# Order of the first panel's products, and late mixes by GpSimd, at both feed-forward starts

## What is computed

```python
def _swiglu(h, w_gate, w_up, w_down):
    return (jax.nn.silu(h @ w_gate) * (h @ w_up)) @ w_down
...
    f = rmsnorm(h, pre_ff_g[l]) @ w_ff1[l]
    f = jnp.square(jax.nn.relu(f)) @ w_ff2[l]
    h = h + rmsnorm(f, post_ff_g[l])
```

## Time and profile before

| what | value |
|---|---|
| median of three runs | 2500.53 us (2500.17 to 2503.38) |
| the profiled execution | 2507.9 us, its span 2505.7 us |
| PE busy | 2392.7 us, 95% of the span |
| DVE busy | 1567.3 us, 63% |
| ACT busy | 1036.3 us, 41% |
| POOL busy | 258.0 us, 10% |
| chain of work that ended last | PE 66%, DVE 3%, DMA 2% |

### The profile page before, as it was taken

How to read it: one execution, slowest core, us unless ns; L and a number is a source line. 1 busy time by engine, 2 the same in 40 slices (tenths; PEclk the granted TensorE clock), 3 DMA queues, 4 the chain that set the end, 5 groups by cost and what they waited for, 6 DMA issues and landing times.

```text
span 2505.7 us, 40944 instructions
## 1 busy us (share of the span) xinstructions
PE 2392.7 (95%) x15691; PEld 2050.3 (82%) x15691; DVE 1567.3 (63%) x2612; ACT 1036.3 (41%) x1972; POOL 258.0 (10%) x253
## 2 busy tenths in 40 slices
PE   5799999999898999999999999999979999999998
PEld 2798888788797888888888898899968888788886
DVE  3632327778768777777668923234287777666677
ACT  1422226676523332332444432433255444444444
POOL 0566310000101000000000100012040000000002
PEclk8899999999998999999999999999989999999999
DMA  9233330000331232232666421110313444477553
GB/s 322 70 118 117 118 84 9 2 2 27 110 127 68 81 126 93 97 125 77 228 198 199 162 68 43 35 35 35 135 68 111 167 139 156 147 256 235 151 176 118
DMA packets 191115, 290.32 MB, mean 116 GB/s; under 512 B 11736, under 2 KB 112028, under 8 KB 190620
## 3 DMA queue, kind: packets, MB, share of 16 engines
q1 hardware_dynamic: 190940, 287.94, 34.7%
HBM read 221.56 MB, written 67.34 MB: 115 GB/s over the span
## 4 chain that ended last, share of the span: by engine, by line
PE 66%; DVE 3%; DMA 2%; issue 1%; POOL 1%; ACT 1%; SPq 0%; POOLq 0%; DVEq 0%; ACTq 0%
PE ps L1519 9%; PE ps L1520 9%; PE ps L1521 9%; PE ps L1761 6%; PE ps L1762 6%; PE ps L1763 6%; PE ps L403 4%; PE ps L404 4%; PE ps L405 4%; PE ps L1982 1%; PE ps L1984 1%; PE ps L1983 1%; PE ps L1411 1%; DMA stage<-w_out 0%; PE ps L2554 0%
## 5 line engine op out<-in xcount | busy, mean ns | idle before, releaser
L403 PE MATMUL ps<-w_hi,ht_hi 128*128 128x256 f32 x1488 | 435.3, 293 | 21.2 <-DVE w_lo L388 14.8
L404 PE MATMUL ps<-w_lo,ht_hi 128*128 128x256 f32 x1488 | 426.6, 287 | 0.0
L405 PE MATMUL ps<-w_hi,ht_lo 128*128 128x256 f32 x1488 | 426.3, 287 | 0.0
L403 PEld LDWEIGHTS ps<-w_hi,ht_hi 128*128 128x128 f32 x1488 | 290.9, 196 | 42.8 <-issue 20.1
L404 PEld LDWEIGHTS ps<-w_lo,ht_hi 128*128 128x128 f32 x1488 | 291.4, 196 | 0.5 <-issue 0.5
L405 PEld LDWEIGHTS ps<-w_hi,ht_lo 128*128 128x128 f32 x1488 | 291.1, 196 | 0.0
L1761 PE MATMUL ps<-ff_b_hi,ff_a_hi 128*128 128x512 f32 x448 | 174.5, 390 | 3.3 <-issue 2.1
L1763 PE MATMUL ps<-ff_b_hi,ff_a_lo 128*128 128x512 f32 x448 | 174.3, 389 | 0.0
L1762 PE MATMUL ps<-ff_b_lo,ff_a_hi 128*128 128x512 f32 x448 | 174.3, 389 | 0.0
L1519 PE MATMUL ps<-ht_hi,swiglu_w_hi 128*128 128x512 f32 x352 | 137.3, 390 | 2.4 <-DVE swiglu_gate L1558 2.4
L1722 ACT ACTIVATE ff_a_hi<-ff_a_raw 128x512 fp32r<-128x512 f32 x112 | 70.7, 631 | 165.9 <-PE ps L1763 148.8
(11 more groups left out here) (371 smaller groups left out, 5792.0 us busy)
## 6 DMA issues: line engine op xcount, KB each, us to landing
ff_a_raw<-ff_act_dram SPq DMA_DIRECT2D x112, 256.0 KB, 2.8
stage<-w_in SPq DMA_DIRECT2D x23, 1024.0 KB, 5.3
swiglu_a_raw<-swiglu_act_dram SPq DMA_DIRECT2D x77, 256.0 KB, 2.9
stage<-w_mod SPq DMA_DIRECT2D x16, 1024.0 KB, 5.4
ff_stage<-w_ff SPq DMA_DIRECT2D x16, 1024.0 KB, 5.5
ff_act_dram<-ff_act_sums SPq DMA_DIRECT2D x16, 1024.0 KB, 4.3
ff_act_dram<-ff_acts SPq DMA_DIRECT2D x16, 768.0 KB, 5.8
swiglu_stage<-w_gate SPq DMA_DIRECT2D x11, 1024.0 KB, 6.3
```

Of the source, the lines that this page charges most:

```text
L403: pe.matmul(bank, a, wh[:, k, :], start=(k == 0), stop=False)
L404: pe.matmul(bank, a, wl[:, k, :], start=False, stop=False)
L405: mm = pe.matmul(bank, b, wh[:, k, :], start=False, stop=(k == KT - 1))
```

## The change

It touches `seven` and the hand-written orders, so both feed-forward starts alike.

- The first panel's products go in the order P1, P2, P3, P5, P7, P6, P4 (`FIRST`; `place_of` turns a product into its count on the semaphores). P3 and P6 swap their weight slots in that panel (`w_at`), and it uses banks 0, 1, 2, 3, 0, 7, 4.
- The five groups of blocks feed P3, P5, P7, P6 and P4 in turn, so the first mixes are turned as g = 1 and 2, and the second mix, P6's, as g = 3 (before as g = 1). Blocks from number 12 on use banks 4 to 6.
- `product_steps` yields after each of a product's four steps, and a block is turned between two: g = 2 within P3, g = 3 within P5, g = 4 within P7 and P6.
- `mix_second`, `mix_third` and the four weight sums of panel 1 move from VectorE to GpSimd (`blocks_pool`, called at the end of `merge_pool` and `leave_pool`).
- `mix_first(2)` and `mix_first(3)` move behind all rows' norms; `mix_first(3)` stands behind three low parts.

The core of the diff (waits and line shifts that follow from the above are left out):

```diff
+        FIRST = (P1, P2, P3, P5, P7, P6, P4)
...
+            def late_at(e):
+                return 4 + (e % 4 if e < 12 else (e - 12) % 3)
...
-            def mix_second(dve, j):
+            def mix_second(pool, j):
                 a, d = half(j, 0), half(4 + j, 1)
-                dve.wait_ge(f.turned, f0.turned + 4 + j + 1)
-                dve.wait_ge(f.mixed, f0.mixed + 2 * j + 2)
-                dve.tensor_tensor(d, d, a, ALU.subtract).then_inc(f.mixed, 1)
+                pool.wait_ge(f.turned, f0.turned + 4 + j + 1)
+                pool.wait_ge(f.mixed, f0.mixed + 8 + j)
+                pool.tensor_tensor(d, d, a, ALU.subtract).then_inc(f.mixed, 1)
...
             def bank(q, b):
+                if q == 0:
+                    return ps[:, (0, 1, 7, 3, 0, 2, 4)[b], :]
                 return ps[:, (7 * q + b) % 4, :]
...
                 if q == 0:
-                    pe.wait_ge(f.lo7, f0.lo7 + {P1: 4, P2: 4, P6: 12, P5: 16, P7: 20, P3: 8, P4: 24}[b])
+                    pe.wait_ge(f.lo7, f0.lo7 + {P1: 4, P2: 4, P3: 8, P5: 12, P7: 16, P6: 20, P4: 24}[b])
...
                 if q + 1 < Q:
                     weight_lo(dve, q + 1, b)
-                    if b in (P1, P2, P6, P5):
+                    if q and b in (P1, P2, P6, P5):
                         weight_sum(dve, q + 1, {P1: 0, P2: 1, P6: 2, P5: 3}[b])
...
-            for g in (1, 2):
-                for j in range(4):
-                    f.turn_block(pe, g, j)
+            for j in range(4):
+                f.turn_block(pe, 1, j)
             pe.wait_ge(dense_evac, evac)
-            f.product(pe, 0, P6)
-            for j in range(4):
-                f.turn_block(pe, 3, j)
-            f.product(pe, 0, P5)
-            for j in range(4):
-                f.turn_block(pe, 4, j)
-            for b in (P7, P3, P4):
-                f.product(pe, 0, b)
+            for k in f.product_steps(pe, 0, P3):
+                f.turn_block(pe, 2, k)
+            for k in f.product_steps(pe, 0, P5):
+                f.turn_block(pe, 3, k)
+            for k in f.product_steps(pe, 0, P7):
+                if k >= 2:
+                    f.turn_block(pe, 4, k - 2)
+            for k in f.product_steps(pe, 0, P6):
+                if k % 2:
+                    f.turn_block(pe, 4, 2 + k // 2)
+            f.product(pe, 0, P4)
...
+        def blocks_pool(pool, f):
+            for j in range(4):
+                f.mix_second(pool, j)
+            for j in range(4):
+                f.mix_third(pool, j)
+            for i in range(4):
+                f.weight_sum(pool, 1, i)
```

More of the change, by code:

```diff
@@ L1406, in turn_block @@
                 else:
-                    pe.wait_ge(f.mixed, f0.mixed + (8 + j + 1, 2 * j + 1, 2 * j + 2, 12 + j + 1)[g - 1])
-                pe.wait_ge(f.lo7, f0.lo7 + (3 + j // 2 if g == 0 else e + 1))
-                source = (half(4 + j, 1), half(4 + j, 1), half(j, 0), half(4 + j, 0), half(j, 1))[g]
+                    pe.wait_ge(f.mixed, f0.mixed + (2 * j + 1, 2 * j + 2, 8 + j + 1, 12 + j + 1)[g - 1])
+                held = [x for x in range(e) if late_at(x) == late_at(e)]
+                pe.wait_ge(f.lo7, f0.lo7 + (3 + j // 2 if g == 0 else 4 + held[-1] + 1))
+                source = (half(4 + j, 1), half(j, 0), half(4 + j, 0), half(4 + j, 1), half(j, 1))[g]
                 for k in range(4):
-                    mm = pe.transpose(ps[:, 4 + e % 4, k * P:(k + 1) * P], source[:, k * P:(k + 1) * P], ident[:, :])
+                    mm = pe.transpose(ps[:, late_at(e), k * P:(k + 1) * P], source[:, k * P:(k + 1) * P], ident[:, :])
                 mm.then_inc(f.turned, 1)
@@ L1890, in blocks_act @@
                     f.block_hi(act, g, j)
-            for b in (P7, P3, P4):
+            for b in (P7, P6, P4):
                 f.weight_hi(act, 0, b)
             f.tick_act(act, 0, P1)
+            for j in range(4):
+                f.block_hi(act, 2, j)
             f.tick_act(act, 0, P2)
-            for g in (2, 3, 4):
+            for g in (3, 4):
                 for j in range(4):
@@ L1904, in blocks_dve @@
         def blocks_dve(dve, f):
+            f.mix_first(dve, 2)
+            for j in range(3):
+                f.block_lo(dve, 0, j)
+            f.mix_first(dve, 3)
+            f.block_lo(dve, 0, 3)
             for j in range(4):
-                f.mix_second(dve, j)
-                f.block_lo(dve, 0, j)
+                f.block_lo(dve, 1, j)
+            f.weight_lo(dve, 0, P7)
             for j in range(4):
-                f.mix_third(dve, j)
-                f.block_lo(dve, 1, j)
-            for b in (P7, P3, P4):
-                f.weight_lo(dve, 0, b)
-            for g in (2, 3, 4):
+                f.block_lo(dve, 2, j)
+            f.weight_lo(dve, 0, P6)
+            f.weight_lo(dve, 0, P4)
+            for g in (3, 4):
                 for j in range(4):
@@ L1936, in first_weights_dve @@
             f.weight_sum(dve, 0, 3)
-            f.weight_lo(dve, 0, P6)
+            f.weight_lo(dve, 0, P3)
             f.weight_lo(dve, 0, P5)
@@ L2163, in merge_dve @@
             f1.weight_sum(dve, 0, 3)
-            f1.weight_lo(dve, 0, P6)
+            f1.weight_lo(dve, 0, P3)
             f1.weight_lo(dve, 0, P5)
```

62 lines of the change are left out of this document (38 added, 24 removed).

## The result

The changed kernel took **2507.45 us** (median of 8 runs, 2503.87 to 2513.81) beside 2502.76 us for the kernel before (8 runs, 2500.17 to 2503.93): a ratio of 1.0022, 95% interval 1.0013 to 1.0030. Slower by 4.7 us, against a forecast of no difference and 2499.9 us; the time lies above the range. A second set gave the same: 2507.95 us (9 runs), ratio 1.0019 (1.0007 to 1.0032).

The account below looks back on a forecast made before the run. TensorE bounds the kernel, so only the two feed-forward starts can gain or lose: -1.3 (SwiGLU), 0.0 (second start), +0.7 (clock) make -0.6 us, 2507.3 profiled, 2499.9 as median; no measured difference, range 2495.5 to 2506.0.

Parts of the forecast that it names:

- P3's earlier entry: Both starts: P3 follows the first transposes instead of P6, 7.2 us sooner in SwiGLU and 4.4 in the second start.
- The new waits: Idle of 1.6 us ahead of P4; 3.7 ahead of the second panel; a weight low part lengthened to about 1.4.
- -1.3 and 0.0: Forecast shift in us of the second panel's first product, in the SwiGLU start and the second feed-forward's start.
- I cost the mixes at nothing: Both starts: GpSimd's mixes hidden by products P3, P5 and P7, showing only from 2.4 us a mix; cost 0.
- 1.7 us of half clock forecast behind P3: SwiGLU start: the first 3.3 us from P3 on run at half clock, adding 1.7 us.
- 1892.0: Second start: time in us given for the last block turned, 17.0 us after P3 at 1875.0.
- the new idle ahead of the second panel: Both starts: 3.7 us idle might drop the clock, 0 to +1.6 us each; taken as 0.
- the base: Whole kernel: profiled 2507.9 us becomes 2507.3; carried to the median of 2500.53, 7.4 lower, it gives 2499.9 us.
- A: Rival, slower: products with blocks between them leave the clock low through P3, P5 and into P7; 2509.6 us; 12%.
- B: Rival, faster: no port lock where it matters, clock stays high or returns at the first product; 2495.4 us; 10%.
- C: Rival: GpSimd's mixes take over 2.4 us each, so the last blocks wait; 2504.7 us at 2.7 each; 3%.
- The product-free stretch in the second start: No product from 1870.4 to 1875.0 us, so the clock may fall: 0 to +1.4 us, taken as +0.7.

Follow-up runs that it names:

- runs 4 and 5: 4: kernel before with only the second panel's four weight sums moved to GpSimd, 2504.16 us; 5: changed kernel with those sums back on VectorE, 2511.28 us.
- run 10: Changed kernel's order and steps, all mixes and sums back on VectorE, second panel's P1 and P2 in spare PSUM banks: 2503.98 us, ratio 1.0006 to before.
- run 8: Kernel before, changed only by putting the second panel's P1 and P2 in spare PSUM banks 4 and 5: 2499.10 us, ratio 0.9984.

## Why the prediction was wrong

**P3's earlier entry: right in its direction and its place, 1.0 us late.** P3 began 18.2 us behind P1 (785.25 less 767.03), where P6 had begun 24.3 behind it; 17.2 was forecast. In the second start it was 13.3 us against 12.7.

**The new waits: right.** 1.6 us forecast ahead of P4, 1.50 and 1.51 measured; 3.7 ahead of the second panel, 3.37 and 3.41; a weight low part of about 1.4 us, 1.47. The lengths of the starts changed by -1.65 and +0.41 us from the trace on which the forecast stood to the first of the changed kernel, and it had said -1.3 and 0.0. That the first came so close is in part luck: P3 came 1.0 us later behind P1 than forecast, and a wait of 0.65 us stood beside GpSimd's mixes, of which the forecast says "I cost the mixes at nothing"; against that, 1.7 us of half clock forecast behind P3 did not come, for the clock was back before it (P3 to P4 took 18.9 us, 20.3 forecast). In the second start the forecast also has a slip of some 0.4 us: 1892.0 is the end of the last block by its own sum and is used as its beginning.

**The step that failed** is the last sentence of the second start: "The same holds for the new idle ahead of the second panel: ... 0 to +1.6 each, I take 0 and keep the ends." It measured 0 and 1.7 us in one trace and 2.8 and 1.7 in the other, so 3.1 us on average where I had 0, beyond the upper end in three of four. I had noted only that 3.7 us is further under the 5.7 at which the clock fell than 4.6 is, and taken that as a reason. It was none: 3.7 is still nearer to 5.7 than to the 1.33 us that left the clock up. Nor is it so that "no row exists" between them. TensorE's waits elsewhere in the same trace are such rows, among them these:

```profile
72.78 0.39 PE L403 MATMUL ps<-w_hi,ht_hi 128*128 128x256 f32 x1 [3.17 <-DVE w_lo L388]
...
85.55 0.58 PE L403 MATMUL ps<-w_hi,ht_hi 128*128 128x256 f32 x1 [3.50 <-DVE w_lo L388]
...
111.85 0.58 PE L403 MATMUL ps<-w_hi,ht_hi 128*128 128x256 f32 x1 [2.95 <-DVE w_lo L388]
```

Low stretches began at 73.9, 84.2 and 111.5. Outside the two starts the trace has ten waits of 2.2 to 5.1 us for which the clock is on record, and it fell at all ten; of six waits of 1.7 to 2.05 us it fell at two. (In other traces such a wait kept its clock now and then, as 2.96 us at 107.2 in the first trace of the changed kernel.) From these rows a low stretch behind both new waits was the likely case, and 0 the unlikely one. And the low stretch is not confined to the idle: it covers the products behind it at half speed, up to 5.6 us of them.

**A second step, mis-sized: the base.** The forecast carried a difference against one profiled execution, 2507.9 us, over to a median 7.4 us lower, as if the excess lay elsewhere. Part of it lay in the very stretch that changes: its two starts took 83.3 us, and 80.7 in the second trace of the same kernel, where the low clock of 1876 to 1883 did not come. Against that execution the starts gain 1.2 us (82.1); against the mean of two traces each they lose 1.0 (83.0 against 82.0), where a gain of 0.6 was forecast. The median itself moved too: 2500.53 us over the three runs that the forecast had, 2502.76 over eight.

**The sum.** 3.1 us of low clock behind the new idle, 1.0 for the starts, and 0.9 for a wait in the down-projection (below) make 5.0 us; the two sets of runs gave 4.7 and 5.0. That it meets them so well is luck: it rests on two traces of each kernel, and the two traced executions of either kernel differ by 7.7 us (2507.9 and 2500.2 before, 2503.9 and 2511.6 changed), part of it in stretches that the change does not touch: the way to the first P1 took 765.7 to 772.7 us over the fourteen traces. The experiments, not this sum, carry the cause. The 7.5 us between the forecast and the result are about these 3.1 and 0.9, 1.6 for the starts (+1.0 where the forecast had -0.6), and 2.2 for the median of before, 7.8 in all.

**The rivals.** A had the price and the sign but the wrong place: the clock was to stay low in the interleaved steps. In all nine traces with those steps it was back between 785 and 793 us and at 1.00 from there to P4. B did not come. C did not as it was put, for GpSimd's mixes took 1.3 to 1.6 us; but beside them blocks did wait for VectorE, 0.6 to 1.1 us in each start.

**The product-free stretch in the second start**, costed at +0.7: no low stretch followed it in any trace of the new order, so its value was 0. In the old order one did, in four traces of five; half of TensorE's busy time in it is 1.6 to 3.3 us each. That is a real gain of the change, and the new idle spends it.

**Left open.** The down-projection of the second feed-forward has a short wait that varies between executions. In the changed kernel it was 2.01 us, and 2.02 in its second trace, and the clock fell at it in both (from 2198.2 to 2201.6 in the first, 1.7 us lost):

```profile
2198.19 0.77 PE L1784 MATMUL ps<-ff_b_hi,ff_a_hi 128*128 128x512 f32 x1 [2.01 <-DVE ff_b_lo L1772]
```

Of the five traces in the old order two had a low stretch there, of the nine in the new order six. By the wait it is eight of the twelve traces in which it lasted about 2.0 us, and neither of the two (runs 4 and 5) in which it was at most 1.4. Whether the change makes it likelier was not tried. Nor is it settled where run 10 loses its time against run 8, and why some starts with 3.1 to 3.4 us of idle kept their clock.

## What to carry to other kernels

When work is pulled forward, look at what it uncovers at the far end: here a 6 us earlier entry ended in a longer wait for one PSUM bank, and other banks for two products (two stood empty) turned a loss of 5 us into a gain of 6.5. Count an idle stretch of TensorE of some 3 us as its own length and then half a low-clock stretch behind it, with a chance of its own, and in a range take in both ends. For that chance look through the whole trace and not only at the stretch that changes: other waits of the same length are the rows that tell. And before a difference from one profiled execution is carried to a median, see whether its excess lies in the stretch that the change touches; a second trace tells.

## What the runs showed of the hardware

The clock fell behind an idle stretch of 3.07 us in one run and stayed up over 3.37 in another, and behind a wait of only 2.01 us in the down-projection it fell as well. The price was paid behind the gap: up to 2.8 us behind gaps of 3.1 to 3.7 us, and up to 3.0 behind those over 5.

Transposes alone sometimes bring the clock back. In the first trace of the changed kernel it rose at 785.0 us, 0.2 us ahead of P3's first matmul, when TensorE had run nothing but transposes since 774.7. In the second trace of the kernel before it rose at 789.0, 4.1 us ahead of P6's first matmul (793.13):

```profile
789.00:790.00 1.00, 0.66 (x5) 0.42 (x4) 1.00 (x2) 0.93 (x2) 0.00 (x0) 0.97 0.00 0
```

In the first trace of that kernel it stayed at 0.50 over transposes for nine us. Over the fourteen traces it rose ahead of that first matmul in seven, by 0.2 to 4.2 us, and behind it in seven. No run here tells what parts them.

A two-input operation of VectorE in SBUF beside GpSimd's sums or mixes was held up in every place where it is shown here: 1.47, 1.77, 2.17 and 2.29 us for 0.68, 0.68, 1.23 and 1.28. Low parts of blocks, which read PSUM, kept their pace beside the mixes (five in 3.07 us from 783.89).

The spread of both kernels' runs is wider than the first sets showed: the kernel before ran from 2496.11 to 2508.05 us over 26 runs, where its first eight spanned 3.8 us.
